# Expert weight blocks in ring slots by kind and parity, and the last two experts' rows returned in one product, gated on their way out of PSUM

## Chip, cores and metric

One core of a Trainium2 chip runs the whole program. The metric is device microseconds of one execution, lower is better. All tensors are 32-bit floats.

## What is computed

Two layers run over 384 tokens (128 context tokens and 256 latent tokens) of width 1024. Each layer mixes the tokens in four head groups and adds the result to the residual x; then comes the mixture of experts, which is what the change touches:

```python
def moe(h, router_w, router_b, w_gate, w_up, w_down):
    ...                       # top-1 of 4 groups, then top-2 experts of 16
    a = jnp.einsum("td,edf->tef", h, w_gate)
    u = jnp.einsum("td,edf->tef", h, w_up)
    z = jax.nn.silu(a) * u * gates[:, :, None].astype(h.dtype)
    return jnp.einsum("tef,efd->td", z, w_down)
...
x  = x + gate2 * MoE(h2)      # gate2 has one row for context, one for latent tokens
```

Each expert has three weight blocks of 2 MB (gate, up, down), so a layer reads 48 blocks. A final RMSNorm follows the second layer.

## The kernel before

**Weights.** Weight blocks pass through six SBUF slots of 2 MB: slots 0 to 3 are the tensor `ring`, slots 4 and 5 are `extra`. SyncE (SP) issues all of them from one queue, in the order of `ISSUE`; before each issue it waits until the block that was last in that slot (`BEFORE`) has been read by TensorE (`block_read`). The expert blocks of a layer are numbered q = 0 to 47. `queued(q)` says which block that is: "a" (gate), "u" (up) or "dn1" (down) of expert e. From q = 8 on the order is a(e), u(e), dn(e-1). The slot is `EXPERT_SLOTS[l][q % 6]`. An issue that waits holds up all that stand behind it. Experts 2 to 15 of the program's order are chosen at run time by load (`ordt`), so SP also reads an expert number before the first block of each.

**Experts.** Token rows are gathered per expert (`xg`, POOL's indirect DMA), turned by TensorE (jobs `xt0`, `xt1`), multiplied with gate and up (job `a`; for a large expert of 96 rows also job `u`), combined by ScalarE and VectorE into `zb`, turned (job `zt`) and multiplied with down (jobs `dn0`, `dn1`). Experts 2, 4, 6, 8, 10 and 12 to 15 are small, of 64 rows: their whole gate and up product is one job `a`. TensorE works by quarters of 32 columns, so the "a" job is 64 matmul records, `u` 32, `dn0` 32, `dn1` 16. Each job name stands for one PSUM bank; bank 3 is `a`, 4 is `dn0`, 5 is `dn1`, 6 is `u`.

**Return of the rows.** The results of experts 0 to 13 go to `ybuf` and are scattered to DRAM (`expert_rows`, POOL L840). Once all are there, SP reads them back, for each third t of the tokens the first pick (`yr[0]`) and the second pick (`yr[1]`), L667. ScalarE multiplies the first pick with a 0/1 factor `kept` (`first_picks`, L1125); VectorE adds the second (`summed`, L1683). The last two experts, 14 and 15 (`LATE`), don't go through DRAM: ScalarE copies their results from PSUM to `ybuf` (L1116, L1117), and TensorE multiplies them with one-hot matrices `late` (64 rows by 128 tokens), two products accumulated for each t and each half b of the columns (job `cm`, L2205, 12 products). VectorE (`completed`) then adds each half from PSUM to the sum (L1691), multiplies with gate2 (`gate`, L1693) and adds to x (L1694). ScalarE forms the sum of squares of x (L871), and VectorE normalizes (`normalize`, L1169 to L1183). In layer 0 TensorE runs nine idle matmuls (`keep_running(9)`, L1733) after the products and then transposes the normalized tokens for the next layer (L1766). In layer 1 the normalization is the final one, with a gain row that POOL loads (L844) and the outputs are stored.

## Time and profile before

| | |
|---|---|
| median of 3 runs | 1264.37 us (1260.73 to 1267.17) |
| profiled execution | 1264.38 us, span 1262.5 us |
| TensorE matmul busy | 1127.8 us (89%), mean granted clock 0.936 |
| VectorE, ScalarE, GpSimd busy | 481.4, 383.9, 234.6 us |
| HBM traffic | 268 GB/s over the span |

The span runs from the first to the last instruction of the profiled execution; 1.9 us lie around it. PE is TensorE, PEld its weight loads, DVE VectorE, ACT ScalarE, POOL GpSimd, SP SyncE; SPq is SP's instruction that issues a DMA. Two stages are DMA-heavy: the experts of layer 0 (about 352 to 617 us from the start) and those of layer 1 (about 968 to 1233 us). In the view of windows the granted clock is 1.00 at 2.4 GHz and 0.50 at 1.2 GHz.

### The profile page before, as it was taken

The numbers are of one execution on the slowest core, as the hardware profiler recorded it, in microseconds if no ns is written. First come the engines' busy times: TensorE is split into PE (matmuls) and PEld (weight loads), VectorE is DVE, ScalarE is ACT, GpSimd is POOL, SyncE is SP. The second block draws the span as 40 slices with busy tenths as digits, with TensorE's granted clock in tenths as the row PEclk, the third lists the DMA queues.
The fourth block names the chain that finished last, engine by engine and source line by source line (L and its number), as shares of the span: only waits on it lengthen the run. The fifth ranks groups of instructions, "written<-read, shape, count | busy, mean of one in ns | idle before, by whom it ended". The sixth has DMA issues, their size and how long they took to land.

```text
span 1262.5 us, 18212 instructions
## 1 busy us (share of the span) xinstructions
PE 1127.8 (89%) x6966; PEld 525.2 (42%) x6966; DVE 481.4 (38%) x1243; ACT 383.9 (30%) x704; POOL 234.6 (19%) x339
## 2 busy tenths in 40 slices
PE   3999989899899888888899999989998998888886
PEld 1555546454433223232354655546444332233332
DVE  1374776734532011110255756675245111111106
ACT  2223444431332212221322334453233322222213
POOL 1231384220011111100200226441101011110100
PEclk9999999889899989998889997997998998999996
DMA  9839631764898999999830313066624899999982
GB/s 365 301 138 178 108 107 67 282 241 173 353 334 341 391 408 399 403 406 399 319 123 17 125 67 100 11 250 221 266 102 173 348 347 407 398 392 400 401 336 102
DMA packets 51213, 325.08 MB, mean 257 GB/s; under 512 B 6710, under 2 KB 7126, under 8 KB 32576
## 3 DMA queue, kind: packets, MB, share of 16 engines
q1 hardware_dynamic: 39296, 293.16, 59.5%
q0 software_dynamic: 10560, 26.17, 8.5%
q10 hardware_dynamic: 1280, 4.72, 0.9%
q8 instruction: 48, 0.79, 0.3%
q14 instruction: 29, 0.24, 0.1%
HBM read 316.15 MB, written 22.25 MB: 268 GB/s over the span
## 4 chain that ended last, share of the span: by engine, by line
PE 61%; DMA 24%; DVE 10%; issue 3%; ACT 1%; SPq 1%; DVEq 0%; ACTq 0%; POOLq 0%
DMA ring<-moe_w_up 19%; PE ps L2094 18%; PE ps L1727 13%; PE ps L1783 7%; PE ps L1984 7%; PE ps L1743 3%; PE ps L2205 3%; DVE attT L1285 2%; PE ps L1766 2%; DMA ring<-ada_w 2%; PE ps L1878 2%; PE ps L1907 1%; PE ps L1733 1%; PE ps L2083 1%; DMA expert_rows<-big,lst 1%
## 5 line engine op out<-in xcount | busy, mean ns | idle before, releaser
L2094 PE MATMUL ps<-ring,dbuf 128*32 128x512 f32 x2336 | 364.2, 609 | 30.8 <-DMA ring<-moe_w_up 22.6
L2094 PE MATMUL ps<-extra,dbuf 128*32 128x512 f32 x1408 | 222.8, 624 | 31.3 <-DMA ring<-moe_w_up 23.5
L2094 PEld LDWEIGHTS ps<-ring,dbuf 128*32 128x32 f32 x2336 | 100.8, 112 | 201.6 <-issue 191.8
L1727 PE MATMUL ps<-ring,extra 128*128 128x512 f32 (+1 forms) x384 | 149.9, 550 | 0.0
L1571 DVE COPY dbuf<-ps 128x256 f32<-128x256 f32 (+1 forms) x32 | 15.4, 483 | 284.3 <-PE ps L2083 284.3
L2094 PEld LDWEIGHTS ps<-extra,dbuf 128*32 128x32 f32 x1408 | 64.9, 114 | 133.9 <-issue 133.7
L1783 PE MATMUL ps<-extra,ring 128*128 128x384 f32 x320 | 107.3, 494 | 0.0
L840 POOL DMA_INDIRECT expert_rows<-big,lst x28 | 26.3, 940 | 421.8 <-ACT big L1117 223.4
L1727 PEld LDWEIGHTS ps<-ring,extra 128*128 128x128 f32 x384 | 74.0, 194 | 69.8 <-issue 66.2
L1984 PE MATMUL ps<-ring,extra 128*128 128x512 f32 x192 | 84.3, 594 | 3.1 <-DVE extra L1460 1.8
L1783 PEld LDWEIGHTS ps<-extra,ring 128*128 128x128 f32 x320 | 60.9, 193 | 41.3 <-issue 2.5
L1743 PE MATMUL ps<-ring,scp 128*32 128x512 f32 x384 | 57.1, 728 | 19.5 <-DMA ring<-ada_w 19.5
L1096 ACT ACTIVATE big<-ps 64x512 f32<-64x512 f32 x18 | 19.2, 1069 | 140.7 <-issue 99.8
L795 POOL DMA_INDIRECT dbuf<-hidden_rows,lst x32 | 31.0, 970 | 165.3 <-DVE lst L1542 131.7
L1285 DVE COPY_PREDICATED attT<-mk,ps 128x128 f32<-128x128 uint16 x168 | 50.5, 300 | 17.3 <-PE ps L1907 11.8
L1984 PEld LDWEIGHTS ps<-ring,extra 128*128 128x128 f32 x192 | 35.7, 190 | 45.1 <-issue 43.4
L931 ACT ACTIVATE big<-ps 128x512 f32<-128x512 f32 (+2 forms) x42 | 21.6, 515 | 107.0 <-PE ps L1727 77.9
L1093 ACT ACTIVATE big<-ps 96x512 f32<-96x512 f32 x14 | 15.1, 1078 | 122.4 <-issue 88.6
L562 POOL TENSOR_TENSOR dbuf<-bbuf 128x128 f32<-128x128 f32 x56 | 25.8, 461 | 118.8 <-PE ps L1907 115.0
L1012 ACT ACTIVATE ring<-ps,small 128x384 f32<-128x384 f32 (+1 forms) x56 | 27.3, 487 | 63.9 <-DVE small L1396 63.1
L2205 PE MATMUL ps<-big,bbuf 64*128 64x512 f32 x48 | 36.6, 941 | 2.9 <-ACT big L1117 2.9
L871 ACT ACTIVATE big<-x 128x1024 f32<-128x1024 f32 x15 | 15.8, 1054 | 65.6 <-DVE x L1694 27.5
(298 smaller groups left out, 1423.8 us busy)
## 6 DMA issues: line engine op xcount, KB each, us to landing
ring<-moe_w_up SPq DMA_DIRECT2D x30, 2048.0 KB, 21.4
ring<-ada_w SPq DMA_DIRECT2D x24, 2048.0 KB, 8.8
ring<-moe_w_down SPq DMA_DIRECT2D x20, 2048.0 KB, 21.7
extra<-moe_w_gate SPq DMA_DIRECT2D x18, 2048.0 KB, 18.0
ring<-moe_w_gate SPq DMA_DIRECT2D x14, 2048.0 KB, 20.5
ring<-w_in SPq DMA_DIRECT2D x12, 2048.0 KB, 20.0
extra<-moe_w_down SPq DMA_DIRECT2D x12, 2048.0 KB, 24.6
ring<-w_out SPq DMA_DIRECT2D x4, 2048.0 KB, 8.2
```

Source lines behind the costliest of these rows:

```text
L562: step(eng.tensor_tensor(strided(out, n * 2 * P + P + m, [-P, 2], [M, nb], [1, m]), right, ref, ALU.subtract))
L795: pool.indirect_dma_start(xg[0:cap, e % 2, :], None, hrow, bass.IndirectOffsetOnAxis(lst[0:cap, e, 0:1], 0), bounds_check=T - 1, oob_is_er ...
L840: pool.indirect_dma_start(yrow, bass.IndirectOffsetOnAxis(lst[0:cap, e - 1, 1:2], 0), ybuf[0:cap, (e - 1) % 2, :], None, bounds_check=2 * ...
L1012: release(act, act.activation(prob[:, i % 2, mp, 0:nk], p[:, 0:nk], ACT.Exp, scale=scale, bias=nmx[:, i % 2, mp:mp + 1], accum_out=sums[:, ...
L1285: ins = dve.copy_predicated(attT[:, 2 * u + h2, :], mk[:, 4 * g + k, :].bitcast(mybir.dt.uint16), p[:, k * P:(k + 1) * P])
L1727: ins = pe.matmul(out, a, b, start=(n == 0), stop=(n == len(pairs) - 1))
L1743: ins = pe.matmul(ps[c:c + 32, MOD_BANK, :], scp[:, 2 * b + k, :], w[:, 2048 * k + 512 * n:2048 * k + 512 * (n + 1)], start=(b == 0 and k ...
L1766: ins = pe.transpose(p[:, n * P:(n + 1) * P], s, ident)
L1783: ins = pe.matmul(p[:, 0:T], w[:, k, c * P:(c + 1) * P], hT[:, k, :], start=(k == 0), stop=(k == KC - 1))
L1984: ins = pe.matmul(p, hT[:, k, t * P:(t + 1) * P], w[:, k, :], start=(k == WO_ORDER[0]), stop=(k == WO_ORDER[-1]))
L2094: return pe.matmul(p[QT * g:QT * (g + 1), :], a, w, start=start, stop=stop, tile_position=(0, QT * g))
L2205: ins = pe.matmul(place_of(("cm", l, t, b)), late[0:cap, j, t, :], ybuf[0:cap, j, b * 512:(b + 1) * 512], start=(j == 0), stop=(j == LATE ...
```

## The change

There are two parts.

**1. Slots.** The slot tables are rewritten so that every kind (gate, up, down) and parity of expert keeps one slot, also at the start of a layer. The two loads of expert 2 change places, the first gate block goes to slot 4 and the first up block to slot 3. Slots 0 and 4 change roles: the gate blocks of even experts are now in slot 4 from expert 0 on, the down blocks of odd experts in slot 0. As slot 4 now holds the last down block of a layer, POOL waits for it before it loads the next layer's caches there.

```diff
-EXPERT_SLOTS = [[3, 4, 5, 1, 2, 0], [3, 4, 5, 1, 2, 0]]
+EXPERT_SLOTS = [3, 0, 5, 1, 2, 4]
+FIRST_PLACES = [5, 0, 2, 3, 4, 1, 5, 0]
+def expert_slot(q):
+    return EXPERT_SLOTS[FIRST_PLACES[q] if q < len(FIRST_PLACES) else q % ESLOTS]
...
-            if q in (5, 7):
-                return ("dn1", 1) if q == 5 else ("a", 2)
+            if 5 <= q <= 7:
+                return (("dn1", 1), ("a", 2), ("u", 2))[q - 5]
...
+                    block_read(pool, ("expert", l - 1, 3 * NE - 1))
```

**2. The last two experts.** ScalarE no longer copies their results. The first piece of the diff is POOL's program, the next three are VectorE's, the last is TensorE's. VectorE multiplies them with gate2 while it reads PSUM (`gated_rows`, four instructions of 64 rows by 512 for each of the two experts, one set for each of the two gate rows s), and puts expert 14 in rows 0 to 63 and expert 15 in rows 64 to 127 of `ybuf`. One product with 128 rows then does for both (6 products in place of 12), and VectorE adds it from PSUM straight to x. The gate product and the addition of the scattered picks are taken by POOL for t = 0 and 1 (two instructions of 128 by 1024 each) and stay on VectorE for t = 2 (`added`). The turning of expert 15's hidden rows is moved into the middle of expert 14's down product, and expert 15's down product gets a bank of its own (`dnz`).

```diff
+                for t in range(NT - 1):
+                    y = yr[0][:, t, :]
+                    pool.wait_ge(s_sum, NT * l + t + 1)
+                    step(pool.tensor_tensor(y, y, gate[:, min(t, 1), :], ALU.mult))
+                    pool.tensor_tensor(x[:, t, :], x[:, t, :], y, ALU.add).then_inc(s_px, 1)
...
+                def gated_rows(j):
+                    job, n = (("dn0", l), NE - 2) if j == 0 else (("dnz", l), 0)
+                    p, r = ready(dve, job, n), slice(SMALL * j, SMALL * (j + 1))
+                    for s in range(2):
+                        for b in range(2):
...
+                            ins = dve.tensor_tensor(late_rows(s)[r, c], p[h], gate[h, s, c], ALU.mult)
...
                 def completed(t):
+                    if t < NT - 1:
+                        dve.wait_ge(s_px, (NT - 1) * l + t + 1)
                     for b in range(2):
-                        y = yr[0][:, t, b * 512:(b + 1) * 512]
-                        release(dve, dve.tensor_tensor(y, y, p, ALU.add), job)
-                    y = yr[0][:, t, :]
-                    step(dve.tensor_tensor(y, y, gate[:, min(t, 1), :], ALU.mult))
-                    dve.tensor_tensor(x[:, t, :], x[:, t, :], y, ALU.add).then_inc(s_x, 1)
+                        job, xs = ("cm", l, t, b), x[:, t, b * 512:(b + 1) * 512]
+                        p = ready(dve, job)
+                        release(dve, dve.tensor_tensor(xs, xs, p, ALU.add), job)
...
-                summed(0)
-                summed(1)
-                expert(NBODY, 0, last=True, next_=False)
-                summed(2)
-                completed(0)
-                completed(1)
-                normalize(2 * l + 2, 0)
-                completed(2)
-                normalize(2 * l + 2, 1)
-                normalize(2 * l + 2, 2)
+                gated_rows(0)
+                summed(0)
+                gated_rows(1)
+                summed(1)
+                completed(0)
+                summed(2)
+                added(2)
+                completed(1)
+                completed(2)
+                for t in range(NT):
+                    normalize(2 * l + 2, t)
...
                 for t in range(NT):
                     for b in range(2):
-                        begin(pe, ("cm", l, t, b))
-                    returned(t, 0)
...
+                        if t == 0 or (t, b) == (1, 0):
+                            pe.wait_ge(s_fold, 3 * l + 2 * s + b + 1)
+                        if (t, b) == (1, 1):
+                            moved(pe, ("dnz", l))
+                        fill(pe.matmul(p, late[:, t, :], late_rows(s)[:, b * 512:(b + 1) * 512], start=True, stop=True), job)
```

ScalarE's part of the tail (`last` is the iteration after expert 15): it makes the copy of expert 15's turned rows, loads its table and then does the three `first_picks`; VectorE makes the copy of expert 14's turned rows.

SP's queue, layer 0, from the load of expert 2 on (the rows with TENSOR_LOAD read an expert number; a wait on a bank is `block_read` on the block that was in the slot). Before:

```order
L625 TENSOR_LOAD ordt [waits bank3_filled]
L625 ISA x2
L627 ISA
L627 DMA extra<-moe_w_gate 128x4096
L627 DMA ring<-moe_w_up 128x4096 [waits bank6_filled]
L627 DMA ring<-moe_w_down 128x4096 [waits bank5_filled]
L625 TENSOR_LOAD ordt [waits bank5_filled]
L625 ISA x2
L627 ISA
L627 DMA ring<-moe_w_gate 128x4096
L627 DMA ring<-moe_w_up 128x4096 [waits bank3_filled]
L627 DMA extra<-moe_w_down 128x4096 [waits bank3_filled]
```

And now:

```order
L646 TENSOR_LOAD ordt [waits bank3_filled]
L646 ISA x2
L648 ISA
L648 DMA extra<-moe_w_gate 128x4096
L648 DMA ring<-moe_w_up 128x4096 [waits bank6_filled]
L648 DMA ring<-moe_w_down 128x4096 [waits bank5_filled]
L646 TENSOR_LOAD ordt [waits bank3_filled]
L646 ISA x2
L648 ISA
L648 DMA extra<-moe_w_gate 128x4096
L648 DMA ring<-moe_w_up 128x4096 [waits bank3_filled]
L648 DMA ring<-moe_w_down 128x4096 [waits bank5_filled]
```

The second TENSOR_LOAD belongs to expert 4's gate block. It waited for bank 5 (the second down product of expert 1) and now waits for bank 3 (job `a` of expert 2); the wait for bank 5 has moved two loads back, to the down block of expert 3.

VectorE's queue at the end of layer 1, from expert 15's product to the last normalization. Before:

```order
L1583 SCALAR_TENSOR_TENSOR big<-big,lst,ps 64x512 x2
L1683 SCALAR_TENSOR_TENSOR big<-bbuf,attT,big 128x1024 x3
L1691 TENSOR_TENSOR big<-big,ps 128x512 x2
L1693 TENSOR_TENSOR big<-big,gate 128x1024
L1694 TENSOR_TENSOR x<-x,big 128x1024
L1691 TENSOR_TENSOR big<-big,ps 128x512 x2
L1693 TENSOR_TENSOR big<-big,gate 128x1024
L1694 TENSOR_TENSOR x<-x,big 128x1024
```

And now:

```order
L1606 COPY dbuf<-ps 128x256
L1612 SCALAR_TENSOR_TENSOR big<-big,lst,ps 64x512
L1729 TENSOR_TENSOR big<-ps,gate 64x512 x4
L1715 SCALAR_TENSOR_TENSOR big<-bbuf,attT,big 128x1024
L1729 TENSOR_TENSOR big<-ps,gate 64x512 x4
L1715 SCALAR_TENSOR_TENSOR big<-bbuf,attT,big 128x1024
L1750 TENSOR_TENSOR x<-x,ps 128x512 x2
L1751 ISA
L1715 SCALAR_TENSOR_TENSOR big<-bbuf,attT,big 128x1024
L1740 TENSOR_TENSOR big<-big,gate 128x1024
L1741 TENSOR_TENSOR x<-x,big 128x1024
L1750 TENSOR_TENSOR x<-x,ps 128x512 x2
```

The eight gate products of the late rows (L1729) stand among the three sums (L1715), one pair of 128x1024 instructions (L1740, L1741) is left where there were three, and the additions from PSUM now go to x.

POOL's queue at the same place, before:

```order
L840 DMA expert_rows<-big,lst 768x1024 x2
L844 DMA ring<-final_norm_g 128x1024
```

And now:

```order
L862 DMA expert_rows<-big,lst 768x1024 x2
L868 TENSOR_TENSOR big<-big,gate 128x1024
L869 TENSOR_TENSOR x<-x,big 128x1024
L868 TENSOR_TENSOR big<-big,gate 128x1024
L869 TENSOR_TENSOR x<-x,big 128x1024
L872 DMA ring<-final_norm_g 128x1024
```

The load of the final gain row now stands behind four vector instructions.

## Rows read from the trace of the kernel before

**Rows 1.** Windows of the experts' stages: stretch, busy by engine, PEclk, DMA share, GB/s.

```profile
392.00:399.00 7.00, 7.00 (x72) 2.62 (x68) 1.37 (x2) 1.18 (x2) 0.93 (x1) 1.00 0.41 108
407.00:520.00 113.00, 97.69 (x860) 32.36 (x856) 14.99 (x23) 27.70 (x39) 13.34 (x14) 0.95 1.01 397
1006.00:1014.00 8.00, 8.00 (x81) 2.87 (x75) 1.37 (x2) 1.18 (x2) 0.87 (x1) 1.00 0.29 65
```

**Rows 2.** Waits of TensorE, 400 to 600 and 1015 to 1215 us: total, times, longest.

```profile
PE ps L2094 <- DMA ring<-moe_w_up: 24.5, 10, 4.4
...
PE ps L2094 <- DMA ring<-moe_w_up: 20.6, 9, 3.5
```

**Rows 3.** Timeline of SP: the gate block of expert 4, layers 0 and 1.

```profile
396.34 0.34 SPq L627 DMA_DIRECT2D ring<-moe_w_gate  x1
...
1011.50 0.33 SPq L627 DMA_DIRECT2D ring<-moe_w_gate  x1
```

**Rows 4.** Chain that ended last: transposes right behind job `a` of expert 2.

```profile
388.41 1.14 PE ps L2083 x12
...
1003.57 1.14 PE ps L2083 x12
```

**Rows 5.** Timeline, end of layer 1, by engine: start, us, engine, line.

```profile
1215.13 0.62 PE L2094 MATMUL ps<-ring,dbuf 128*32 128x512 f32 x2 [1.08 <-DMA ring<-moe_w_up]
...
1229.31 3.64 PE L2094 MATMUL ps<-ring,dbuf 128*32 128x512 f32 x32 [1.34 <-ACT dbuf L1099]
...
1236.27 15.37 PE L2205 MATMUL ps<-big,bbuf 64*128 64x512 f32 x20 [1.40 <-ACT big L1117]
...
1230.76 1.15 ACT L1125 ACTIVATE big<-big,attT 128x1024 f32<-128x1024 f32 x1 [1.55 <-DMA bbuf<-expert_rows]
...
1236.54 1.15 ACT L1125 ACTIVATE big<-big,attT 128x1024 f32<-128x1024 f32 x1 [0.32 <-DMA bbuf<-expert_rows]
...
1255.95 1.28 DVE L1181 SCALAR_TENSOR_TENSOR big<-x,small,ring 128x1024 f32<-128x1024 f32 x1
...
1258.12 1.28 DVE L1181 SCALAR_TENSOR_TENSOR big<-x,small,ring 128x1024 f32<-128x1024 f32 x1
```

**Rows 6.** Timeline, end of layer 0, TensorE and VectorE.

```profile
599.17 0.62 PE L2094 MATMUL ps<-ring,dbuf 128*32 128x512 f32 x2
...
637.66 9.67 PE L1733 MATMUL ps<-const 128*128 128x512 f32 x18
...
643.80 0.75 DVE L1183 TENSOR_SCALAR big<-x,small 128x1024 f32<-128x1024 f32 x1
...
647.16 2.78 PE L1766 MATMUL ps<-const,big 128*128 128x128 f32 x24
```

**Rows 7.** Window in the products of layer 1; chain's piece behind TensorE's longest wait.

```profile
1240.00:1243.00 3.00, 3.00 (x5) 1.10 (x4) 2.93 (x3) 0.00 (x0) 0.00 (x0) 0.50 0.00 0
...
583.95 9.98 PE ps L2094 x64
```

**Rows 8.** Single lines: duration in ns, least, median, most.

```profile
L787 POOL TENSOR_TENSOR big<-big x2: 1802/1804/1805, 278.6 to 893.1; 128x768 f32<-128x768 f32 x2
...
L1691 DVE TENSOR_TENSOR big<-big,ps x12: 679/686/689, 623.3 to 1251.7; 128x512 f32<-128x512 f32 x12
...
L1694 DVE TENSOR_TENSOR x<-x,big x6: 1224/1224/1226, 626.2 to 1253.7; 128x1024 f32<-128x1024 f32 x6
```

**Rows 9.** Timeline: a POOL instruction and VectorE instructions that fall into it.

```profile
178.66 4.53 POOL L755 TENSOR_TENSOR extra<-extra,const 128x2048 f32<-128x2048 f32 x1 [2.69 <-DMA extra<-skew_rows]
...
181.07 2.14 DVE L1396 TENSOR_SCALAR small<-small 128x2 f32<-128x2 f32 x1
...
795.20 0.17 DVE L1396 TENSOR_SCALAR small<-small 128x2 f32<-128x2 f32 x1
```

**Rows 10.** DMA issues of the page: KB, us from issue to landing.

```profile
y_sample<-big SPq DMA_DIRECT2D x2, 512.0 KB, 2.6
...
ring<-final_norm_g POOLq DMA_DIRECT2D x1, 512.0 KB, 9.9
```

More of the change, by code:

```diff
@@ L107 @@
 for l in range(L):
-    for blk, slot in list(zip(PRE[l], MIX_SLOTS[l])) + [(("expert", l, q), EXPERT_SLOTS[l][q % ESLOTS]) for q in range(3 * NE)]:
+    for blk, slot in list(zip(PRE[l], MIX_SLOTS[l])) + [(("expert", l, q), expert_slot(q)) for q in range(3 * NE)]:
         BEFORE[blk] = LAST_IN.get(slot)
@@ L1108, in expert @@
                         act.activation(by_chunk(sU)[0:2 * QT], in_rows(p)[2 * QT:P], ACT.Copy).then_inc(s_half, 1)
-                    if not first:
+                    if not first and next_:
                         p = ready(act, ("dn0", l), e - 1)
@@ L1571, in turned_out, with expert @@
                     release(dve, dve.tensor_copy(rows_turned(at, cap)[:, 0:4, :], turned_rows(p, cap)), ("xt0", l), e)
-                def expert(i, es, first=False, last=False, next_=True):
+                def expert(i, es, first=False, next_=True):
                     e = i * EXP_PER_BODY + es
@@ L1577, in expert @@
                         turned_out(e + 1, (es + 1) % 2, cap_of(i, es + 1))
-                    if not last and cap_of(i, es) == SMALL:
+                    else:
+                        p, cap = ready(dve, ("zt", l), e - 1), cap_of(i, es - 1)
+                        release(dve, dve.tensor_copy(products_turned(cap), turned_rows(p, cap)), ("zt", l), e - 1)
+                    if cap_of(i, es) == SMALL:
                         p = ready(dve, ("a", l), e)
@@ L1584, in expert @@
                                                               op0=ALU.mult, op1=ALU.mult), ("a", l), e)
-                    elif not last:
+                    else:
                         n_u = use_of("u", i, es)
@@ L2124, in expert, with turn_products @@
                         fill(ins, ("a", l), e)
-                    if not first:
-                        moved(pe, *product_of(l, i, es - 1))
-                        turn("zt", e - 1, [zb[0:CAP, f * P:(f + 1) * P] for f in range(FC)])
+                    def turn_products(es):
+                        moved(pe, *product_of(l, i, es))
+                        turn("zt", i * EXP_PER_BODY + es, [zb[0:CAP, f * P:(f + 1) * P] for f in range(FC)])
+                    if not first and not last:
+                        turn_products(es - 1)
                     if next_:
```

88 lines of the change are left out of this document (53 added, 35 removed).

## Prediction

> **What bounds the kernel now.** I read the windows first, then the waits and the chain of waits, then the timelines of the two stretches that the change touches.
>
> In the experts' stages the DMA engines are the bound: from 407 to 520 us their share is 1.01 at 397 GB/s, while TensorE is busy 97.69 of 113 us [rows 1]. TensorE waits for an up block ten times in layer 0 (24.5 us in all) and nine times in layer 1 (20.6 us) [rows 2]. So whatever lets the stream of weights start sooner moves the whole stage. There is one hole in each stream, near its start: from 392 to 399 us the share is 0.41 (108 GB/s), from 1006 to 1014 us 0.29 (65 GB/s) [rows 1]. It ends with the issue of expert 4's gate block at 396.34 and 1011.50 us [rows 3]. That block stood in slot 0 behind expert 1's second down product; two more loads are queued behind it.
>
> At the end of a layer the bound is another one. I call A the start of expert 15's job `a`: 599.17 us in layer 0 [rows 6], 1215.13 in layer 1 [rows 5]. In layer 1 the first pick is multiplied at A + 15.6, on its landing, the third at A + 21.4 (1236.54) [rows 5]. TensorE's last 20 records of the 24 for the late rows begin at A + 21.1 and take 15.37 us, up to A + 36.5 [rows 5], at the half clock (0.50, 1.2 GHz) [rows 7]. VectorE follows them with three passes for each t and ends at 1258.12 + 1.28, which is A + 44.3 [rows 5]. In layer 0 the idle matmuls run from 637.66 for 9.67 us and the transposes for the next layer begin at 647.16, A + 48.0 [rows 6].
>
> **Part 1, the slots.** Expert 4's gate block now waits for job `a` of expert 2. The transposes behind that job begin at 388.41 and 1003.57 us [rows 4]; SP then reads an expert number, so I put the issue 0.5 us later, at 388.9 and 1004.1: before the stream runs dry at 392 and 1006. Expert 4's up block waited for the same job already and follows at once. Together they are 4 MB, 10.6 us of stream at 397 GB/s, and expert 3's down block, which now waits for expert 1's product, is issued at about 396 and 1011 us, well before they have landed. So the hole closes. Its worth has two bounds. By share it is 7 x (1 - 0.41) = 4.1 us and 8 x (1 - 0.29) = 5.7 us; by bytes, 7 x (1 - 108/397) = 5.1 and 8 x (1 - 65/397) = 6.7. The sums are 9.8 and 11.8; the drain of a stream is partly latency, so I take **10.8 us**. The end of each stage follows in full, as TensorE's waits on the stream in each layer (24.5 and 20.6 us) are far more than that. If they were not, the gain would stop at the waits that are left; that they come again within a few experts is what hides TensorE's own time.
>
> The swap of expert 2's two loads costs nothing: both are read by one job. The release of slot 0 for the next layer's fourth projection block comes sooner; I count nothing, since the first dense stage starts long after it. POOL's new wait and its cache loads go behind the tail; they are wanted far into the next layer.
>
> **Part 2, TensorE's side.** Expert 15's turn now stands inside expert 14's down product, and VectorE makes expert 14's copy at once, where ScalarE did it behind a SiLU. Before, expert 15's down product ran from A + 14.2 for 3.64 us, up to A + 17.8 [rows 5]. The turn (a third of a transposing group of 1.14 us [rows 4]) and the wait of 1.34 us in front of that product [rows 5] fall away: it ends at about A + 16.0. The six products with 128 rows are 12 records instead of 24. They start once VectorE has gated the first block, and by the count below TensorE is never the last from there on.
>
> **Part 2, VectorE and POOL.** Prices: a VectorE instruction of 512 columns with PSUM 0.69 us, one of 1024 columns from SBUF 1.22 [rows 8], a sum of picks like the final gain 1.28 [rows 5], one normalization 2.17 in layer 1 (1255.95 to 1258.12) [rows 5], and 2.17 - 1.28 + 0.75 = 1.64 in layer 0 [rows 6]. The trace has no POOL instruction of 128x1024; L787 has two full inputs and 768 columns, 1804 ns [rows 8], which gives 2.41.
>
> What happens when both run at once decides the rest. At 181.07 us a VectorE instruction on two columns takes 2.14 us where it takes 0.17 otherwise; it ends at 183.21, and the POOL instruction beside it at 178.66 + 4.53 = 183.19 [rows 9]. So VectorE can be held until POOL's instruction is done. I take it that this holds for the sums, the gate product and the addition on VectorE, and not for the instructions that read PSUM. Then, from A in layer 1:
>
> - sum 0 ends at 16.8 (first pick multiplied) + 1.3 + latency = 18.2. POOL's pair for t = 0: 18.2 to 23.0. VectorE gates expert 15's rows meanwhile, 18.2 to 21.0; TensorE's first product can start at 18.9.
> - sum 1 is ready at 21.0 but held until 23.0, and ends at 24.3. The additions for t = 0 end at 25.7.
> - POOL's gate product for t = 1: 24.3 to 26.7. Sum 2 is held until then and ends at 28.0. POOL's addition: 28.0 to 30.4.
> - VectorE's gate product and addition for t = 2, held until 30.4, end at 32.9; additions for t = 1 and t = 2 at 34.3 and 35.7; three normalizations of 2.17 and some latency, 42.6.
>
> That is **1.7 us** before A + 44.3. In layer 0 the normalizations are shorter, and the transposes start at about A + 41.0 instead of A + 48.0: 7.0 us. But TensorE is done with the idle matmuls by A + 32 to A + 38 (12 + 18 records of 0.43 to 0.77 us from 18.9), and then waits 3 to 9 us. After its wait of 4.4 us, 64 records took 9.98 us [rows 7], where 32 at full clock take 3.64 [rows 5]: 2.7 us lost. I take 2.0. So layer 0's tail gives **5.0 us**.
>
> The Trainium skill bears on this, in the page "SBUF — State Buffer", section "Who interferes with whom": a VectorE instruction with two SBUF inputs and a GpSimd instruction that reads SBUF take turns on one read port, and whoever comes second is fully blocked. By that rule the tail is as in the list above; the trace agrees so far, with 2.14 us against 0.17.
>
> **Sum.** 10.8 + 5.0 + 1.7 = 17.5 us from the profiled execution's 1264.38, which is also the median of the runs: 1246.9, say 1247.
>
> **The rivals.**
>
> *No holding between VectorE and POOL.* The row of 2.14 us is one instruction of another kind. If the two overlap freely, sum 1 ends at 22.4, the additions for t = 0 at 24.4, sum 2 at 25.7, VectorE's pair for t = 2 at 28.2 (POOL's t = 1 at 27.8), the last addition at 31.0 and the last normalization at 37.9: 4.7 us less in each layer, 1247 - 9.4 = 1237.5. Chance 0.2.
>
> *The hole is only shifted.* SP has one queue, and expert 3's down block now sits two places further back on an old wait. If the stream runs dry there, or the slots come free later than it wants, half or more of the 10.8 us is lost: 1252 to 1257. Against it, 10.6 us of stream are queued when that wait ends. Chance 0.13.
>
> *The final gain row comes late.* Its load stands behind POOL's four instructions: issue at A + 30.4, wanted by VectorE at A + 36.6. The load took 9.9 us beside the weights, while a store of the same size into an idle system took 2.6 [rows 10]. With 2.6 nothing waits; with 9.9 and its issue of 0.6, the tail grows by 4.3 us, to 1251. I take nothing, as the stream is over by then. Chance 0.09.
>
> *Slower.* TensorE's clock stays at 1.2 GHz after the wait that layer 0's tail now has, into the dense products of layer 1. In the late products it did stay at 0.50 with TensorE busy [rows 7]. Every us at the half clock on dense work loses half a us: 35 us of it eat up the 17.5, and from 48 us on the kernel is slower by over 0.5%; with 60 us it would be 1247 + 30 = 1277. Against it, after the wait of 4.4 us only 2.7 us were lost in all [rows 7]. Chance 0.03.
>
> **The numbers.** The forecast, 1247, has 0.55. Its own unknowns (hole 9.8 to 11.8, clock 0 to 2.9, POOL's instruction some tenths either way, eight times) make it 1243 to 1251. The range reaches to the free overlap below and into the shifted hole above: 1236 to 1255. A measurement of this kernel tells about 0.5%, 6.3 us, from no change. Below 1258 lie the forecast and nearly all of the first three rivals: faster 0.93. Within 0.5% lie a hole that stays whole with a late gain row, or some 20 to 45 us at the half clock: 0.04. Slower 0.03.
>
> **What the profile would show.** In layer 0 and layer 1, expert 4's gate block issued right behind job `a` of expert 2, and windows there at a share of 1.0; if the share falls later, the hole has moved. At each end: the sums L1715 and the pair L1740, L1741 begun or stretched to the end of a POOL instruction; if they last 1.22 to 1.28 us while POOL is busy, there is no holding. Layer 0's transposes about 41 us behind expert 15's job `a`, with TensorE idle before them and its clock at 0.50 for a few us; the last normalization of layer 1 about 42.6 us behind it. The forecast is wrong if a VectorE instruction waits for the gain row, if the stream is not the bound of the experts once the hole is closed, or if the picks come back from DRAM at another time.

## The result

| | before | after |
|---|---|---|
| median | 1262.55 us (1257.65 to 1267.17, 4 runs) | 1248.19 us (1245.33 to 1250.38, 4 runs) |
| profiled execution | 1264.38 us, span 1262.5 us, clock 0.936 | 1250.38 us, span 1248.7 us, clock 0.944 |

The ratio is 0.9873, with a 95% interval of 0.9838 to 0.9909: 16.0 us faster, with an interval of 11.5 to 20.5 us (the medians themselves differ by 14.4 us). A second measurement (e7 below) gave 0.9882 (0.9824 to 0.9939). 1247 us was predicted. All ratios here compare fast runs alone, so the one beside e7 leaves out e7's execution of 2209.27 us and three of before's 11, from 1269.65 to 1271.50 us.

### The profile page after: what moved, and what is told of

Its sections match the earlier page's. It is cut to its first block, busy times and chain, and to the rows that moved or that the text cites. A ratio compares the mean times of both kernels' runs of the same rounds, so it can differ in the third digit from the quotient of the medians.

```text
span 1248.7 us, 18191 instructions
## 1 busy us (share of the span) xinstructions
PE 1103.9 (88%) x6942; PEld 521.5 (42%) x6942; DVE 491.3 (39%) x1259; ACT 379.0 (30%) x694; POOL 255.7 (20%) x347
## 4 chain that ended last, share of the span: by engine, by line
PE 58%; DMA 24%; DVE 13%; issue 3%; ACT 1%; SPq 0%; DVEq 0%; ACTq 0%; POOLq 0%
DMA ring<-moe_w_up 19%; PE ps L2152 17%; PE ps L1785 14%; PE ps L1841 7%; PE ps L2042 7%; PE ps L1801 3%; PE ps L1824 2%; DVE attT L1311 2%; DMA ring<-ada_w 2%; PE ps L1936 2%; PE ps L2141 2%; PE ps L1965 1%; DVE dbuf L1287 1%; DMA expert_rows<-big,lst 1%; DMA bbuf<-expert_rows 1%
## 5 line engine op out<-in xcount | busy, mean ns | idle before, releaser
L2152 PE MATMUL ps<-ring,dbuf 128*32 128x512 f32 x2432 | 416.1, 601 | 39.2 <-DMA ring<-moe_w_up 27.4
L2152 PE MATMUL ps<-extra,dbuf 128*32 128x512 f32 x1312 | 242.9, 612 | 16.1 <-DMA ring<-moe_w_up 15.5
L2152 PEld LDWEIGHTS ps<-ring,dbuf 128*32 128x32 f32 x2432 | 114.3, 111 | 232.0 <-issue 216.7
L1785 PE MATMUL ps<-ring,extra 128*128 128x512 f32 (+1 forms) x384 | 152.4, 557 | 0.0
L1841 PE MATMUL ps<-extra,ring 128*128 128x384 f32 x320 | 110.4, 504 | 0.0
L817 POOL DMA_INDIRECT dbuf<-hidden_rows,lst x32 | 31.2, 974 | 165.3 <-DVE lst L1568 131.9
L1124 ACT ACTIVATE big<-ps 64x512 f32<-64x512 f32 x18 | 19.3, 1070 | 146.2 <-issue 105.9
L2042 PEld LDWEIGHTS ps<-ring,extra 128*128 128x128 f32 x192 | 35.7, 190 | 45.0 <-issue 43.4
L1618 DVE TENSOR_TENSOR big<-big,ps 64x512 f32<-64x512 f32 x14 | 9.5, 680 | 65.6 <-ACT big L1132 65.6
L1629 DVE COPY big<-ps 64x512 f32<-64x512 f32 x14 | 9.7, 693 | 64.1 <-PE ps L2152 64.1
## 6 DMA issues: line engine op xcount, KB each, us to landing
extra<-moe_w_down SPq DMA_DIRECT2D x2, 2048.0 KB, 16.4
```

Source lines behind the costliest of these rows:

```text
L817: pool.indirect_dma_start(xg[0:cap, e % 2, :], None, hrow, bass.IndirectOffsetOnAxis(lst[0:cap, e, 0:1], 0), bounds_check=T - 1, oob_is_er ...
L1785: ins = pe.matmul(out, a, b, start=(n == 0), stop=(n == len(pairs) - 1))
L1841: ins = pe.matmul(p[:, 0:T], w[:, k, c * P:(c + 1) * P], hT[:, k, :], start=(k == 0), stop=(k == KC - 1))
L2042: ins = pe.matmul(p, hT[:, k, t * P:(t + 1) * P], w[:, k, :], start=(k == WO_ORDER[0]), stop=(k == WO_ORDER[-1]))
L2152: return pe.matmul(p[QT * g:QT * (g + 1), :], a, w, start=start, stop=stop, tile_position=(0, QT * g))
```

## The profile after

Two groups of the page, the weight products (L2094 before). Columns: instructions, busy us, mean ns, idle time ahead and what ended it.

```profile
L2152 PE MATMUL ps<-ring,dbuf 128*32 128x512 f32 x2432 | 416.1, 601 | 39.2 <-DMA ring<-moe_w_up 27.4
L2152 PE MATMUL ps<-extra,dbuf 128*32 128x512 f32 x1312 | 242.9, 612 | 16.1 <-DMA ring<-moe_w_up 15.5
```

TensorE still waits for up blocks, 27.4 + 15.5 = 42.9 us over the whole execution. The same two groups of the page before show:

```profile
L2094 PE MATMUL ps<-ring,dbuf 128*32 128x512 f32 x2336 | 364.2, 609 | 30.8 <-DMA ring<-moe_w_up 22.6
L2094 PE MATMUL ps<-extra,dbuf 128*32 128x512 f32 x1408 | 222.8, 624 | 31.3 <-DMA ring<-moe_w_up 23.5
```

That is 46.1 us (the 45.1 us of [rows 2] are of two windows only). The stream of weights is still the bound of the experts.

**The hole.** SyncE's issues, from the timelines of the same two places as [rows 3]:

```profile
399.05 0.34 SPq L648 DMA_DIRECT2D extra<-moe_w_gate  x1
399.48 0.37 SPq L648 DMA_DIRECT2D ring<-moe_w_up  x1
405.49 0.33 SPq L648 DMA_DIRECT2D ring<-moe_w_down  x1
...
1001.08 0.33 SPq L648 DMA_DIRECT2D extra<-moe_w_gate  x1
1001.52 0.38 SPq L648 DMA_DIRECT2D ring<-moe_w_up  x1
1007.24 0.33 SPq L648 DMA_DIRECT2D ring<-moe_w_down  x1
```

And the windows there (columns as in [rows 1]; the last two are the DMA share and GB/s):

```profile
392.00:399.00 7.00, 7.00 (x69) 2.49 (x62) 0.92 (x2) 0.61 (x1) 1.92 (x2) 1.00 1.01 425
396.00:404.00 8.00, 7.33 (x76) 2.99 (x72) 1.30 (x2) 2.22 (x4) 0.12 (x1) 1.00 1.01 393
404.00:408.00 4.00, 4.00 (x44) 1.52 (x40) 1.37 (x2) 1.02 (x2) 0.15 (x1) 1.00 1.00 389
1002.00:1010.00 8.00, 8.00 (x77) 2.84 (x73) 1.65 (x3) 1.44 (x3) 0.41 (x1) 1.00 1.02 370
407.00:520.00 113.00, 101.02 (x920) 34.95 (x912) 15.40 (x24) 29.46 (x41) 13.38 (x14) 0.98 1.01 397
```

In this profile the experts of layer 0 start 9.9 us later than in before's, so what was at 392 to 399 us there is at about 402 to 409 us here; the rows cover both. The share is 1.0 where it was 0.41 and 0.29, and 1.01 later on as before. Nothing has moved behind.

**The end of layer 0.** TensorE's timeline from expert 15's job `a`, the point called A in the prediction (start, duration, and what ended the idle time):

```profile
604.16 0.62 PE L2152 MATMUL ps<-ring,dbuf 128*32 128x512 f32 x2 [1.20 <-DMA ring<-moe_w_up]
...
616.42 3.62 PE L2152 MATMUL ps<-extra,dbuf 128*32 128x512 f32 x32
621.91 5.39 PE L2274 MATMUL ps<-big,bbuf 128*128 128x512 f32 x12 [1.87 <-DVE big L1729]
627.13 7.89 PE L1791 MATMUL ps<-const 128*128 128x512 f32 x18
643.48 4.73 PE L1824 MATMUL ps<-const,big 128*128 128x128 f32 x24 [8.46 <-DVE big L1209]
```

The transposes start at A + 39.3 (before A + 48.0, [rows 6]). TensorE is idle for 8.46 us ahead of them, and they take 4.73 us where they took 2.78. What VectorE and GpSimd do meanwhile, from their two timelines:

```profile
623.55 2.35 POOL L869 TENSOR_TENSOR x<-x,big 128x1024 f32<-128x1024 f32 x1
627.07 2.36 POOL L868 TENSOR_TENSOR big<-big,gate 128x1024 f32<-128x1024 f32 x1 [1.16 <-DVE big L1715]
629.50 3.21 POOL L869 TENSOR_TENSOR x<-x,big 128x1024 f32<-128x1024 f32 x1
```

```profile
619.76 1.28 DVE L1715 SCALAR_TENSOR_TENSOR big<-bbuf,attT,big 128x1024 f32<-128x1024 f32 x1
621.08 2.85 DVE L1729 TENSOR_TENSOR big<-ps,gate 64x512 f32<-64x512 f32 x4
624.30 2.69 DVE L1715 SCALAR_TENSOR_TENSOR big<-bbuf,attT,big 128x1024 f32<-128x1024 f32 x1 [0.37 <-ACT big L1151]
627.02 1.41 DVE L1750 TENSOR_TENSOR x<-x,ps 128x512 f32<-128x512 f32 x2
628.54 1.97 DVE L1715 SCALAR_TENSOR_TENSOR big<-bbuf,attT,big 128x1024 f32<-128x1024 f32 x1
630.54 3.25 DVE L1740 TENSOR_TENSOR big<-big,gate 128x1024 f32<-128x1024 f32 x1
633.83 1.22 DVE L1741 TENSOR_TENSOR x<-x,big 128x1024 f32<-128x1024 f32 x1
```

Set the ends side by side. GpSimd's instructions end at 625.90, 629.43 and 632.71 us; VectorE's sums at 626.99 and 630.51 and its gate product at 633.79: 1.08 or 1.09 us later each time. The same instructions take 1.28 and 1.22 us when GpSimd is idle. So VectorE is held until GpSimd's instruction ends. Each of the three began inside the GpSimd instruction behind whose end it ends. It works both ways: GpSimd's last addition takes 3.21 us instead of 2.35, as it began during a sum; it ends 2.20 us behind that sum's end at 630.51. The instructions that read PSUM (L1729, L1750) keep their 2.85 and 1.41 us beside a busy GpSimd.

**The end of layer 1.** The same engines, rows of the timeline of all engines:

```profile
1219.47 1.15 ACT L1151 ACTIVATE big<-big,attT 128x1024 f32<-128x1024 f32 x1 [2.16 <-DMA bbuf<-expert_rows]
1220.73 1.28 DVE L1715 SCALAR_TENSOR_TENSOR big<-bbuf,attT,big 128x1024 f32<-128x1024 f32 x1 [0.37 <-ACT big L1151]
...
1222.87 7.09 PE L2274 MATMUL ps<-big,bbuf 128*128 128x512 f32 x12 [2.21 <-DVE big L1729]
...
1224.93 3.02 DVE L1715 SCALAR_TENSOR_TENSOR big<-bbuf,attT,big 128x1024 f32<-128x1024 f32 x1
...
1229.51 1.96 DVE L1715 SCALAR_TENSOR_TENSOR big<-bbuf,attT,big 128x1024 f32<-128x1024 f32 x1
...
1231.51 3.25 DVE L1740 TENSOR_TENSOR big<-big,gate 128x1024 f32<-128x1024 f32 x1
1233.62 0.62 POOL L872 DMA_DIRECT2D ring<-final_norm_g  x1
...
1244.39 1.28 DVE L1207 SCALAR_TENSOR_TENSOR big<-x,small,ring 128x1024 f32<-128x1024 f32 x1
```

A is 1204.79 us here. The first pick is multiplied at A + 14.7 (before A + 15.6), the last normalization ends at 1245.67, A + 40.9 (before A + 44.3). The gain row (L872) is issued at 1233.62 and lands 3.9 us later by the page, at about 1237.5; the first normalization that reads it starts at 1240.06, and VectorE doesn't wait for it.

## The experiments

All twelve profiles (ten kernels, and before and after a second time each) are cut at the same points: the start of layer 0's experts, A, the first transpose for layer 1 (T), the start of layer 1's experts, A again, and the end of the last normalization. Each entry is the difference of two points in a timeline, one profile each; before, for example: 353.31, 599.17, 647.16, 968.46, 1215.13 and 1258.12 + 1.28 us.

| profile | up to experts | experts 0 | A to T | T to experts 1 | experts 1 | A to end |
|---|---|---|---|---|---|---|
| before | 353.3 | 245.9 | 48.0 | 321.3 | 246.7 | 44.3 |
| e8, before again | 360.7 | 247.5 | 45.7 | 320.9 | 245.8 | 47.5 |
| e3, order alone | 353.5 | 241.5 | 45.6 | 320.9 | 241.9 | 45.9 |
| e1, part 1 alone | 359.4 | 241.9 | 40.5 | 317.7 | 240.6 | 44.6 |
| e2, part 2 alone | 361.1 | 244.8 | 39.5 | 318.5 | 245.8 | 42.2 |
| e9, part 2 and order | 357.5 | 242.2 | 39.4 | 323.5 | 242.1 | 42.2 |
| after | 363.2 | 241.0 | 39.3 | 321.4 | 239.9 | 40.9 |
| e7, after again | 360.4 | 240.3 | 39.3 | 323.0 | 240.2 | 40.6 |
| e4, longer idle run | 361.3 | 241.3 | 39.4 | 323.0 | 239.7 | 40.8 |
| e5, nothing on GpSimd | 360.6 | 241.3 | 40.0 | 325.7 | 240.6 | 41.3 |
| e10, one third on GpSimd | 361.0 | 241.1 | 39.1 | 323.4 | 239.5 | 42.1 |
| e6, additions left out | 358.2 | 242.5 | 36.3 | 323.5 | 241.6 | 37.8 |

**e1: part 1 alone.** The kernel before with the new slots.

```diff
-EXPERT_SLOTS = [[3, 4, 5, 1, 2, 0], [3, 4, 5, 1, 2, 0]]
+EXPERT_SLOTS = [3, 0, 5, 1, 2, 4]
+FIRST_PLACES = [5, 0, 2, 3, 4, 1, 5, 0]
...
-            if q in (5, 7):
-                return ("dn1", 1) if q == 5 else ("a", 2)
+            if 5 <= q <= 7:
+                return (("dn1", 1), ("a", 2), ("u", 2))[q - 5]
...
+                    block_read(pool, ("expert", l - 1, 3 * NE - 1))
```

> Part 1 alone (slots by kind and parity, POOL's wait for the last block), the end of the layers as before. Theory (the hole near the start of each experts' stage closes and the stages end sooner by its size): 10 to 12 us faster than before, about 1252, with windows at a DMA share of 1.0 right behind the issue of expert 4's gate block, and the stretch from expert 0's job a to expert 15's job a shorter by 4 to 5 us in layer 0 and 6 to 7 in layer 1. Rival (the hole is only shifted): under 5 us faster, with a low share a few windows later.

**e2: part 2 alone.** The changed kernel with the old slots.

```diff
-EXPERT_SLOTS = [3, 0, 5, 1, 2, 4]
-FIRST_PLACES = [5, 0, 2, 3, 4, 1, 5, 0]
...
+EXPERT_SLOTS = [[3, 4, 5, 1, 2, 0], [3, 4, 5, 1, 2, 0]]
...
-            if 5 <= q <= 7:
-                return (("dn1", 1), ("a", 2), ("u", 2))[q - 5]
+            if q in (5, 7):
+                return ("dn1", 1) if q == 5 else ("a", 2)
...
-                    block_read(pool, ("expert", l - 1, 3 * NE - 1))
```

> Part 2 alone (late rows gated out of PSUM, POOL's share), the slots as before. Theory: the hole stays as before, and the two ends of the layers give what they gave in the changed kernel: about 8.5 us in layer 0 and 3.4 in layer 1 by its profile, 1251 against 1263. The two parts add up to the change. Rival (they don't add, because the earlier stream also brings the scattered rows back sooner): under 8 us faster.

**e3: the order alone.** The kernel before with its slots; two entries of SyncE's order change places, so that expert 4's up block goes ahead of its gate block.

```diff
+    rest = [("expert", l, q) for q in range(4, 3 * NE)]
+    rest[11 - 4], rest[12 - 4] = rest[12 - 4], rest[11 - 4]
...
-    ISSUE.append(body + [("expert", l, q) if isinstance(q, int) else q for q in late_blocks] + [("expert", l, q) for q in range(4, 3 * NE)])
+    ISSUE.append(body + [("expert", l, q) if isinstance(q, int) else q for q in late_blocks] + rest)
```

> The kernel before with one thing changed: SP issues expert 4's up block ahead of its gate block, so that one load stands in the queue that need not wait for expert 1's second down product. No slot is changed. Theory (the hole is the head of the queue waiting): the first missing load comes 7.5 us sooner, 2 MB or 5.3 us of stream, so most of the hole closes: 8 to 11 us faster than before. Rival (the gain of part 1 lies in the new slots themselves, at the border of the layers for instance): within 3 us of before.

**e4: a longer idle run.** The changed kernel with more idle matmuls ahead of layer 0's transposes.

```diff
-                    keep_running(9)
+                    keep_running(19)
```

> The changed kernel with 19 instead of 9 idle matmuls behind the late products of layer 0, so that TensorE has 8.6 us more of them and goes on until the normalized tokens are there. Theory (the clock falls in that wait of 8.5 us and the transposes and first products behind it run slower): the 24 transposes take 2.8 us instead of 4.7, and the kernel is 1.5 to 3 us faster than the changed one, 1246. Rival (the clock's fall there costs nothing behind the transposes): the same time within noise. Slower by 1 us or more if the idle matmuls now run beyond the tokens.

Measured together, with before at 1262.97 us (1255.21 to 1272.94, 29 runs):

| | median | ratio | gain, us |
|---|---|---|---|
| e1 | 1253.77 (1248.65 to 1262.78) | 0.9935 [0.9906, 0.9964] | 8.2 (4.5 to 11.9) |
| e2 | 1256.99 (1252.21 to 1261.96) | 0.9967 [0.9944, 0.9991] | 4.2 (1.1 to 7.1) |
| e3 | 1255.84 (1246.70 to 1260.75) | 0.9940 [0.9910, 0.9970] | 7.6 (3.8 to 11.4) |
| e4 | 1247.32 (1243.86 to 1250.28) | 0.9879 [0.9847, 0.9911] | 15.3 (11.2 to 19.3) |

The sum of the parts, 8.2 + 4.2 = 12.4 us, lies in the interval of both together (16.0, from 11.5 to 20.5), so the parts may add up; the noise is too large to say it closer. Against what was expected, e1's median is 1.8 us too slow and its interval reaches 10 to 12 us; its two stages are 4.0 and 6.1 us shorter than in before, as expected. e2 missed: about 12 us were expected and 4.2 measured, at most 7.1, which is the number of its rival (under 8 us). Its ends of layers did shrink, to 39.5 and 42.2 us, and its hole stayed, as the theory had it. What the rival gave as a reason, scattered rows that return sooner with the earlier stream, is small at most: with the earlier stream the tails are 39.4 and 42.2 us in e9, 39.3 and 40.9 in after. What else took the rest is taken up in the next section, under the sum. e3's 7.6 us are just under the 8 to 11 expected, and its rival (within 3 us of before) is outside its interval. e3 is as good as e1 within the noise: the runs show no worth of the new slots beyond the closed hole, since two entries of the order close it as well. In the windows of 4 us at that place e2 keeps the hole, and e3 has none. Of e2, from 396 us:

```profile
396.00:400.00 4.00, 3.34 (x36) 1.84 (x36) 1.30 (x2) 2.06 (x3) 0.00 (x0) 1.00 0.76 290
400.00:404.00 4.00, 4.00 (x41) 1.44 (x37) 0.54 (x1) 1.18 (x2) 0.00 (x0) 1.00 0.06 17
404.00:408.00 4.00, 4.00 (x44) 1.56 (x40) 0.83 (x2) 0.00 (x0) 1.91 (x2) 1.00 0.75 242
```

Of e3, from 392 us:

```profile
392.00:396.00 4.00, 4.00 (x40) 1.42 (x36) 0.04 (x1) 1.18 (x2) 0.00 (x0) 1.00 0.98 339
396.00:400.00 4.00, 4.00 (x44) 1.50 (x40) 1.34 (x2) 0.00 (x0) 1.44 (x2) 1.00 0.98 398
400.00:404.00 4.00, 4.00 (x44) 1.90 (x40) 0.38 (x1) 1.18 (x2) 0.46 (x1) 1.00 0.99 419
```

e2's hole is 4 x (0.24 + 0.94 + 0.25) = 5.7 us of the stream. e4's transposes run at full speed again, in the group of layer 0:

```profile
L1824 PE MATMUL ps<-const,big 128*128 128x128 f32 x24 | 2.8, 275 | 0.0
```

They start no later (T at A + 39.4). Yet the time is that of the changed kernel, as its rival had it, and the stage from T to the next experts is 1.6 us longer than in after's first profile, and equal to its second. The 2 us that the fallen clock costs there could not be turned into time that these runs can tell from noise.

**e5: nothing on GpSimd.** The changed kernel, with GpSimd's gate products and additions given to VectorE.

```diff
-                for t in range(NT - 1):
-                    y = yr[0][:, t, :]
-                    pool.wait_ge(s_sum, NT * l + t + 1)
-                    step(pool.tensor_tensor(y, y, gate[:, min(t, 1), :], ALU.mult))
-                    pool.tensor_tensor(x[:, t, :], x[:, t, :], y, ALU.add).then_inc(s_px, 1)
...
-                    if t < NT - 1:
-                        dve.wait_ge(s_px, (NT - 1) * l + t + 1)
...
                 summed(1)
+                added(0)
                 completed(0)
                 summed(2)
-                added(2)
+                added(1)
                 completed(1)
+                added(2)
```

> The changed kernel with one edit: GpSimd's two gate products and two additions for the tokens t=0 and t=1 are given to VectorE, which then does them between its sums. Theory (the two engines hold each other: in the changed kernel's trace the sums are 2.69 and 1.97 us and the gate product 3.25 us where they are 1.28 and 1.22 us alone, +4.1 us in layer 0 and about +4.4 us in layer 1): the holding goes, VectorE gets 4 operations of about 1.23 us more, 4.9 us a layer. The end of a layer is 0.5 to 0.8 us later than now, the time within 2 us of the changed kernel (about 1249). Rival (no holding; the long sums have another cause and stay long): 4.9 us more in each layer, about 1258.

**e6: the additions left out.** The same removal from GpSimd's program, with nothing given to VectorE: the scattered picks of two thirds of the tokens are not gated and not added to x.

> The changed kernel with GpSimd's gate products and additions for the tokens t=0 and t=1 left out, so that the rows gathered for these two thirds of the tokens are not added to x: a part of the computation is missing. Theory (VectorE is slowed by GpSimd working beside it): VectorE's sums fall to 1.28 us each and its gate product to 1.22 us, and both ends of layers are shorter by about 4 us, the time is about 1240. Rival (VectorE waits for PSUM or for the gathered rows, not for GpSimd): the sums stay at 2 to 3 us, the time within 1 us of the changed kernel.

Measured together, with before at 1268.33 us (1250.69 to 1271.50, 11 runs): e5 1251.73 us (1245.57 to 1254.50), ratio 0.9889 [0.9834, 0.9943]; e6 1240.70 us (1235.53 to 1246.48), ratio 0.9811 [0.9754, 0.9868]. VectorE's timeline of e6 in layer 0:

```profile
621.24 1.28 DVE L1709 SCALAR_TENSOR_TENSOR big<-bbuf,attT,big 128x1024 f32<-128x1024 f32 x1 [0.63 <-ACT big L1145]
622.56 1.41 DVE L1742 TENSOR_TENSOR x<-x,ps 128x512 f32<-128x512 f32 x2
624.77 1.28 DVE L1709 SCALAR_TENSOR_TENSOR big<-bbuf,attT,big 128x1024 f32<-128x1024 f32 x1 [0.80 <-ACT big L1145]
626.09 1.23 DVE L1734 TENSOR_TENSOR big<-big,gate 128x1024 f32<-128x1024 f32 x1
```

With GpSimd quiet the sums are 1.28 us and the gate product 1.23. This settles the cause of the long instructions. The tails shrink by 3.0 us each (39.3 to 36.3; 40.8, the mean of after's two, to 37.8), not 4: VectorE now waits 0.63 and 0.80 us for the picks instead. In e5 the tails are 0.7 and 0.5 us longer than in after (40.0; 41.3 against 40.8), as the 0.5 to 0.8 of the theory and far from the rival's 4.9. Its time was expected within 2 us of the changed kernel; its median is 2.4 us above e7's, of the same measurement, but the ratios (0.9889 and 0.9882) are 0.9 us apart. What the change gives to GpSimd costs VectorE about as much in holding as it would cost it in work.

**e7 and e8: after and before once more.** No edit.

> The changed kernel once more, for a second profile and more executions. Theory (the length of layer 0 before the experts, 353.3 us in the profile of before and 363.2 us in that of after, varies with the windows in which the clock falls, from one execution to the next, and not with the kernel): it is anything from 353 to 363 us here, with the time in step, and the median ratio stays at 0.987 to 0.988. Rival (the change lengthens that stage): 360 us or more again.

> The kernel before once more, one profile. Theory (chance decides how often the clock falls ahead of the experts): their start may lie anywhere from 353 to 363 us, and the products of 64 rows at the end of layer 0 may run at 1.2 GHz (17 us, as in the first profile) or at 2.4 GHz (10.6 us, as in the profile with the slots alone). Rival (both belong to the kernel): 353 us and 17 us again.

e7 measured 1249.37 us in the median of six (five of them from 1248.20 to 1250.36), ratio 0.9882 [0.9824, 0.9939]. It needs 360.4 us up to its experts, which is what its rival had, that the change lengthens this stage. e8's one execution took 1272.79 us, nearly the longest of before (1272.94). It shows that the kernel before can be as slow there: 360.7 us up to its experts instead of 353.3. The clock goes with it. Windows from 126 to 262 us, first of before, then of e8 (the third column from the end is the granted clock):

```profile
126.00:262.00 136.00, 123.68 (x673) 71.42 (x674) 97.58 (x302) 59.78 (x149) 59.23 (x102) 0.94 0.50 146
```

```profile
126.00:262.00 136.00, 126.05 (x664) 74.18 (x662) 92.32 (x295) 58.89 (x145) 58.65 (x102) 0.90 0.49 146
```

It is 0.94 and 0.90; in the same window of after it is 0.87. All twelve profiles fall in line. From the start to the experts the granted clock is 0.96 in the two that take 353 us (before, e3), 0.95 in e9 (357.5), 0.94 in e1 and e6 (359.4 and 358.2), and 0.93 in the seven that take 360.4 to 363.2 us. From T to the next experts it is 0.95 in e1 (317.7), 0.92 in e5 (325.7), e6 and e9 (323.5 both), and 0.93 or 0.94 in the rest, in between. So the length of these two stages goes with the clock, and e8 shows that one kernel can have either. Whether the change moves the odds is not shown: of the eight profiles with part 2 six have 0.93 in the first stage, of the four without it one.

The late products of 64 rows ran at half speed in e8 too, so e8 doesn't settle whether that is chance or belongs to the kernel. Of e8, e3 and e1, the groups of layer 0 (least, middle and most ns, and from when to when):

```profile
L2205 PE MATMUL ps<-big,bbuf x24: 589/1057/1057, 626.0 to 643.5; 64*128 64x512 f32 x24
```

```profile
L2207 PE MATMUL ps<-big,bbuf x24: 588/1057/1058, 612.8 to 630.3; 64*128 64x512 f32 x24
```

```profile
L2214 PE MATMUL ps<-big,bbuf x24: 588/590/694, 620.7 to 630.7; 64*128 64x512 f32 x24
```

From the first start to the last, these 24 took 17 to 20 us in before, e8 and e3; in e1 they took 10, and A to T was 40.5 us without part 2. The granted clock is 0.50 from 621 to 637 us in before and 1.00 from 621 to 631 us in e1. In e1 they came without a gap behind expert 15's down product, in before the last 20 came after a wait of 1.51 us for ScalarE's copy, in e8 and e3 after 0.88 and 0.87. In layer 1 they ran at half speed in e1 too, 15.89 us for 20 after a wait of 1.19 us. So the wait for the copy is the suspect, but no run took it away alone, and it stays one. e1's layer 0 differs in another way as well: job `a` of expert 15 came after a wait of 2.80 us for its block, and its first matmuls took 1.04 us.

**e9: part 2, and the order in place of the slots.** The edits of e2 and e3 together.

```diff
-EXPERT_SLOTS = [3, 0, 5, 1, 2, 4]
...
+EXPERT_SLOTS = [[3, 4, 5, 1, 2, 0], [3, 4, 5, 1, 2, 0]]
...
+    rest = [("expert", l, q) for q in range(4, 3 * NE)]
+    rest[11 - 4], rest[12 - 4] = rest[12 - 4], rest[11 - 4]
...
```

> Part 2 of the change on the old slots, with two entries of SyncE's order swapped in the place of part 1 (expert 4's up block ahead of its gate block). Theory (part 1 is worth only what the hole near each stage's start cost, and the swap closes it as well: in the profile of the swap alone the experts took 241.5 and 241.9 us up to expert 15's job a, as in the kernels with the new slots, against 245 to 247.5 us without either): both parts add up, the time is that of the changed kernel, 1248 to 1250 us, the two stages 240 to 242.5 us, the two tails about 39.5 and 41 us. Rival (the new slots do more than close the hole): one of the stages stays at 244 us or more and the time is 1252 us or more.

**e10: one third on GpSimd.** GpSimd keeps t = 0 and VectorE takes t = 1.

```diff
-                for t in range(NT - 1):
+                for t in range(1):
...
-                    if t < NT - 1:
-                        dve.wait_ge(s_px, (NT - 1) * l + t + 1)
+                    if t == 0:
+                        dve.wait_ge(s_px, l + 1)
...
                 summed(1)
+                added(1)
                 completed(0)
```

> The changed kernel with GpSimd taking the gate product and addition of t=0 alone; those of t=1 are given to VectorE, ahead of its additions for t=0. Theory (the two engines hold each other, so that work given to GpSimd costs VectorE nearly what it would cost it to do it): the last sum falls to 1.28 us and the gate product of t=2 to 1.22 us, VectorE does 2.45 us more, the last normalization of layer 1 ends 40.4 us behind expert 15's job a where it is 40.5 to 40.9 now; the time is within 2 us of the changed kernel. Rival (no holding): 2.4 us more in each tail, 43 us behind job a.

Measured together, with before at 1265.13 us (1253.31 to 1272.06, 11 runs): e9 1251.45 us (1247.50 to 1254.86), ratio 0.9892 [0.9845, 0.9939]; e10 1248.05 us (1242.98 to 1250.84), ratio 0.9856 [0.9810, 0.9901]. e9's two stages, 242.2 and 242.1 us, speak for the theory (the rival wanted 244 or more in one); its time lies between the two cases, and its interval covers after's ratio, 0.9873. In e10 the last sum takes 1.28 us and the gate product of t = 2 1.22 us, as the theory had them, and the tail of layer 0 is 39.1 us against 39.3 in after (the rival wanted 2.4 us more). Its last tail is 42.1 us, not 40.4, nearer to the rival's 43, and by that number the theory missed. The loss is ahead of VectorE's part, though. Expert 15's down product:

```profile
1204.07 0.92 PE L2153 MATMUL ps<-ring,dbuf 128*32 128x512 f32 x2 [2.81 <-DMA ring<-moe_w_up]
...
1218.03 1.47 PE L2153 MATMUL ps<-extra,dbuf 128*32 128x512 f32 x12
```

It starts 13.96 us behind job `a`, in after 12.26 (1217.05 - 1204.79). Job `a` came after a wait of 2.81 us here and its first matmuls take 0.92 us; in after the wait was 1.12 and they take 0.62. From the start of that product to the end of the last normalization e10 needs 1246.13 - 1218.03 = 28.1 us, after 28.6 and e7 28.3. e2 and e9 bear it out: there too job `a` came after a wait of 2.8 us, and their last tails are 42.2 us. e10's ratio, 0.9856, is the lowest of a complete kernel, but its interval covers after's, and no complete kernel of the set is measurably better than the changed one.

## Why the prediction was right

**What bounds it.** Right. The experts stay bound by the stream, and what the stream gains TensorE gains.

**Part 1, 10.8 us.** Right in mechanism and size. The mean of the first stage is 246.1 us in the three profiles with the hole (before, e8, e2) and 241.5 in the nine without; of the second 246.1 and 240.7. That is 4.6 + 5.4 = 10.0 us, at the bound worked out from the share (4.1 + 5.7). The latency for which I went above it didn't show. Over its 12 executions part 1 alone was worth 8.2 us (4.5 to 11.9). Of the steps, the issue came 0.85 and 1.12 us behind the transposes (398.20 and 999.96 us), not 0.5, and expert 3's down block 6 us behind the pair; neither let the stream run dry.

**Part 2, layer 0, 5.0 us.** A to T was predicted as 41.0 and measured as 39.3; the wait of TensorE was put at 3 to 9 us and was 8.46; the clock's loss was put at 2.0 us and was 4.73 - 2.78 = 1.95 (the granted clock is 0.57 from 643.5 to 648 us and 1.00 from 648 to 660). The idle matmuls ended at A + 30.9, a little ahead of the A + 32 to A + 38 given; the upper end of that was also summed too low, since 18.9 and 30 records of 0.77 us make 42.0. Against the profile before the tail gained 8.7 - 1.95 = 6.7 us. Against all four profiles with the old end (48.0, 45.7, 45.6, 40.5: mean 45.0) A to T gained 5.6. **The term that was mis-sized is the base**: the 48.0 was the longest of four, with the late products at 1.2 GHz nearly throughout. Between 40.5 and 48.0 the old end depended on the clock, and the new one, with half the products and never the last to finish, does not (39.3 to 39.5 in five profiles).

**Part 2, layer 1, 1.7 us.** Too small: 3.4 us against the profile before, and 45.6 - 41.3 = 4.3 between the means (before, e8, e3, e1 against e2, e9, after, e7, e4). Of these 2.6 us too little 1.3 are the base again, 44.3 being the shortest of four with a mean of 45.6. The other 1.3 are the new end, 42.6 as counted against a mean of 41.3 (40.9 in after), and there two terms were too long. The first pick was multiplied at A + 14.7, where I took A + 15.6 from before. It was at A + 14.9 in e1, which has part 1 alone; over all profiles it is at 14.9 to 16.4 without part 2 and at 14.1 to 15.2 with it, so part 2 may have a share in it, which no run separates. And the holds: their order was as counted, but I had sum 1 ending at 24.3, sum 2 at 28.0, the gate product and addition of t = 2 at 32.9 and the last addition at 35.7; measured were 23.2, 26.7, 31.2 and 34.2. The difference grows from 1.1 to 1.7 us mostly because a held instruction is not all still to do when it is let go (1.08 us are left of 1.22 to 1.28), which I had not counted at any of the three holds.

**The holding.** Right, and shown by e6: sums of 2.69, 3.02 and 1.97 us beside GpSimd, 1.28 without. GpSimd's instruction took 2.35 us, 2.41 was the estimate. The Trainium skill, "SBUF — State Buffer", section "Who interferes with whom", states that a VectorE instruction with two SBUF inputs contends with a GpSimd instruction that reads SBUF, and that one with at most one SBUF input, outside the two-port modes, does not. The rows above agree on both sides, with the held sums and products and with the undisturbed 1.41 us of the additions from PSUM. The row of 2.14 us from which the prediction took the holding [rows 9] did not bear on that rule: its instruction reads one SBUF tensor. It showed that VectorE can be held, not by which pairs.

**The sum.** 17.5 us was forecast, with the clock's 2.0 us taken off the tail of layer 0. In the table that loss falls behind T, so like for like the three forecast gains are 10.8 + 7.0 + 1.7 = 19.5 us. By the means of the stages they are 10.0 + 5.6 + 4.3 = 19.9. Two stages that the change does not touch take some back. From T to the next experts it is 320.2 us in the four profiles with the old end and 322.8 in the eight with the new, 2.6 us. I had 2.0 there, for the slower transposes; but they are not the cause of the difference: e1 has them (4.51 us) in the shortest stage of all, 317.7, and e4 has transposes of 2.8 us at 323.0. Up to the first experts it is 356.7 against 360.4, 3.7 us, on which the prediction put nothing. There e8 shows 7.4 us of difference for one and the same kernel, so 3.7 us between means of four and eight may be chance. Against pure chance stands e2, part 2 alone in 12 executions: 4.2 us, at most 7.1, where the tails by the means give 5.6 + 4.3 = 9.9. Both stages go with the granted clock, as e8 showed; whether part 2 lowers it is open, and so is what these 6.3 us are due to. In the one pair of profiles compared first the first stage took back 9.9 us, which nearly hid that each touched stage of that pair had gained more than forecast. The mechanisms of both parts were right; that the number is so close is in part luck. The gain was forecast as 17.5 us and is 14.4 between the medians, 3.1 less; the time misses by 1.2 us only, because before's median is 1262.55 us and not the 1264.38 from which I subtracted. Among the terms 1.4 us too much in layer 0 and 0.8 in part 1 stand against 2.6 too little in layer 1, and about 4 us in the two untouched stages were not in the sum.

**The rivals.** No holding: refuted by e5 and e6. The hole only shifted: refuted by the shares of 1.0. The gain row late: it was issued 6.4 us ahead of its use, landed in 3.9 and nothing waited. The clock staying low into the dense products: it cost 1.95 us in the transposes and was back at 1.00 for the products behind them.

## What to carry to other kernels

Look for the one place in a stream of loads where the share drops, and ask which wait stands at the head of the queue: two entries in another order were worth as much as a new slot table. Work given to GpSimd saved VectorE 0.5 to 0.7 us of 4.9 here, as both engines then worked on SBUF operands at once; what it did beside VectorE's PSUM reads cost nothing. A tail in which TensorE has short waits has no single length (40.5 to 48.0 us here): take its base from several profiles before pricing what removes it. And check the stages that a change does not touch: by the means they took back a third here of what the touched ones gained, and the cause is open.
